# A hybrid decoder step: where the expert router's scores are formed on TensorE and copied on ScalarE

## The reference

```python
q = (xblk @ wq).reshape(PEER_BLOCK, PEER_HEADS, 2, D_HALF)
sc = jnp.einsum('thpc,hpnc->thpn', q, keys)              # scores: 2 x 128 of each token and head
s_top, i_top = lax.top_k(sc, PEER_TOPK)
cand = s_top[..., 0, :, None] + s_top[..., 1, None, :]   # 16 x 16 candidates
best, pos = lax.top_k(cand, PEER_TOPK)                   # the 16 experts
gates = jax.nn.softmax(best, axis=-1)
act = jax.nn.gelu(einsum('thkd,td->thk', u_tab[experts], xblk))
y = einsum('thk,thkd->td', gates * act, v_tab[experts])
```

## Time and profile before

| | us |
|---|---|
| median of 3 runs | 3481.84 |
| lowest to highest | 3478.89 to 3486.58 |
| the profiled execution | 3499.93 |
| its span on the core | 3498.0 |

### The profile page before, as it was taken

How to read it: one execution, slowest core, us unless ns; L and a number is a source line. 1 busy time by engine, 2 the same in 40 slices (tenths; PEclk the granted TensorE clock), 3 DMA queues, 4 the chain that set the end, 5 groups by cost and what they waited for, 6 DMA issues and landing times.

```text
span 3498.0 us, 31532 instructions
## 1 busy us (share of the span) xinstructions
PE 1883.2 (54%) x9976; PEld 885.6 (25%) x9976; DVE 2019.9 (58%) x5131; ACT 705.2 (20%) x1970; POOL 2059.3 (59%) x2211
## 2 busy tenths in 40 slices
PE   6996876766645772644354444444444544444433
PEld 2463543333312220421121111111111211121200
DVE  2337645566677665655655665565566655655563
ACT  2122112221223221112111211121111111111111
POOL 1324546666655555656666666666666666666664
PEclk9998988878766896876676666766666666666666
DMA  9638999999998999989999999999999999999997
GB/s 351 218 111 304 368 331 396 385 391 398 347 376 303 367 369 396 373 331 365 365 359 356 374 365 375 341 372 369 366 361 358 375 362 357 356 369 359 360 363 304
DMA packets 393188, 1228.50 MB, mean 351 GB/s; under 512 B 54563, under 2 KB 104719, under 8 KB 389678
## 3 DMA queue, kind: packets, MB, share of 16 engines
q0 software_dynamic: 305728, 1109.92, 83.6%
q1 hardware_dynamic: 46314, 75.12, 6.1%
q10 hardware_dynamic: 40980, 41.44, 3.6%
HBM read 1211.31 MB, written 16.04 MB: 351 GB/s over the span
## 4 chain that ended last, share of the span: by engine, by line
POOL 33%; issue 20%; another core or an unknown queue 16%; PE 11%; DVE 9%; DMA 7%; ACT 3%; DVEq 2%; ACTq 0%; SPq 0%; POOLq 0%
POOL arena L529 16%; POOL arena L518 16%; DVE arena L1558 5%; DMA arena<-in_peer_v,eid 3%; PE PS L725 3%; DMA arena<-in_peer_u,eid 2%; PE PS L855 2%; PE PS L668 1%; DMA arena<-in_w_ada 1%; PE PS L685 1%; PE PS L825 1%; ACT arena L1171 1%; DMA arena<-in_w_in 1%; PE PS L776 0%
## 5 line engine op out<-in xcount | busy, mean ns | idle before, releaser
L1558 DVE CUSTOM_DVE_ANT_0 arena<-arena,PS 128x1024 f32<-128x1024 f32 x1056 | 1241.9, 1215 | 770.5 <-DMA arena<-in_peer_u,eid 360.6
L855 PE MATMUL PS<-arena 128*32 128x512 f32 x4224 | 853.1, 892 | 1220.0 <-DMA arena<-in_peer_v,eid 754.2
L529 POOL DMA_INDIRECT arena<-in_peer_v,eid x1040 | 982.6, 945 | 840.2 <-remote 366.0
L518 POOL DMA_INDIRECT arena<-in_peer_u,eid x1056 | 998.9, 946 | 408.5 <-issue 313.3
L855 PEld LDWEIGHTS PS<-arena 128*32 128x32 f32 x4224 | 172.3, 141 | 1697.8 <-issue 1549.6
L685 PE MATMUL PS<-arena 128*128 128x256 f32 (+1 forms) x576 | 193.9, 498 | 102.9 <-ACT arena L1047 42.6
L1171 ACT ACTIVATE arena<-sel,wgt 128x32 f32<-128x32 f32 x1056 | 231.0, 310 | 35.5 <-issue 18.9
L1154 ACT ACTIVATE arena<-PS 128x256 f32<-128x256 f32 (+1 forms) x48 | 17.1, 357 | 932.3 <-remote 805.9
L825 PE MATMUL PS<-arena 128*128 128x128 f32 x1280 | 172.5, 293 | 26.2 <-issue 26.2
L825 PEld LDWEIGHTS PS<-arena 128*128 128x128 f32 x1280 | 161.4, 205 | 74.0 <-issue 73.7
L685 PEld LDWEIGHTS PS<-arena 128*128 128x128 f32 x576 | 124.0, 221 | 185.9 <-issue 51.4
(11 more groups left out here) (241 smaller groups left out, 1976.9 us busy)
## 6 DMA issues: line engine op xcount, KB each, us to landing
arena<-in_w_ada SPq DMA_DIRECT2D x24, 1024.0 KB, 11.4
arena<-in_peer_u,eid POOLq DMA_INDIRECT x1056
arena<-in_peer_v,eid POOLq DMA_INDIRECT x1056
arena<-in_peer_wq ACTq DMA_DIRECT2D x10, 1024.0 KB
arena<-in_peer_wq SPq DMA_DIRECT2D x4, 2048.0 KB, 47.7
arena<-in_w_in SPq DMA_DIRECT2D x14, 512.0 KB, 9.8
arena<-in_w_in ACTq DMA_DIRECT2D x14, 512.0 KB
arena<-in_x_prompt ACTq DMA_DIRECT2D x8, 512.0 KB, 5.1
```

The source lines that it names most:

```text
L518: po.indirect_dma_start(out=Ur[:, k % RING, :], out_offset=None, in_=a["peer_u"], in_offset=bass.IndirectOffsetOnAxis(ap=eid[m % 4][:, k:k ...
L529: po.indirect_dma_start(out=Vr[:, k % RING, :], out_offset=None, in_=a["peer_v"], in_offset=bass.IndirectOffsetOnAxis(ap=eid[m % 4][:, k:k ...
L855: last = mm(PS[j * GT:(j + 1) * GT, half, :], dsel[m % 2][:, k, :], rows[:, k % RING, half * 512:(half + 1) * 512], start=m % 2 == 0 and q ...
L1558: last = ve.tensor_tensor_reduce(out=Ur[:, k % RING, :], in0=Ur[:, k % RING, :], in1=hP, scale=1.0, scalar=0.0, op0=ALU.mult, op1=ALU.add, ...
```

## The change

Two lists change, TensorE's and ScalarE's. From unit 24 on TensorE forms the scores of unit n + 2 at the head of its round n, behind the transposes in an even round and ahead of group 0, and no longer between groups 2 and 3. In rounds 22 and 23 they stay where they were. ScalarE copies the scores ahead of the query in every round from 24 on, and no longer behind it; round 23 keeps its order.

```diff
@@ TensorE, round n
                 if n % 2 == 0 and 0 < n < UNITS:
                     replicate(n // 2)
+                if FIRST <= n and n + 2 < UNITS:
+                    scores(n + 2)
                 for q in range(NV):
...
-                    if q == NV - 1 and FIRST <= n + 2 < UNITS:
+                    if q == NV - 1 and n in (FIRST - 2, FIRST - 1):
                         scores(n + 2)
                     if q == NV - 1 and n == FIRST - 1 or q == 1 and n >= FIRST and t < TT:
                         queries(t, h)
@@ ScalarE, round n
-                if n >= FIRST and t < TT:
-                    take_queries(t, h)
                 if FIRST <= n + 2 < UNITS:
                     take_scores(n + 2)
-                if n == FIRST - 1:
+                if n >= FIRST - 1 and t < TT:
                     take_queries(t, h)
                 if n + 1 < UNITS:
                     exps(n + 1)
```

## The result

| | us |
|---|---|
| before, median of 20 runs | 3469.62 (3454.7 to 3486.86) |
| after, median of 20 runs | 3493.04 (3468.13 to 3509.89) |
| ratio, 95% interval | 1.0053 (1.0037 to 1.007) |
| the profiled execution after, its span | 3468.13, 3466.3 |

The change makes the kernel 0.5% slower, some 18 us by the ratio; the two medians lie 23 us apart. The forecast was 3486 with 0.34 on "within 0.2%"; the range of 3430 to 3530 holds the result, and it fell in the case that had 0.37.

The account below looks back on a forecast made before the run. It took a loop of V gather, landing, weighing, late signal and next gather, 92.7 us a pair, as the bound. Terms 0 + 0 + 4 = +4 us on the median 3481.84 gave 3486 us, range 3430 to 3530.

Parts of the forecast that it names:

- the case that had 0.37: Whole kernel: the outcome "slower", beyond the 0.2% counted as the same; its chance was 0.37.
- about 12 us: GpSimd: its waits in each pair of rounds, said to stand ahead of the first of four V gathers.
- ScalarE, 0 us: Scores copy at the head ends the Gelu's 3.5 us lateness, but VectorE still waits for replicated queries: 0 us.
- Rival (c): The Gelu's lateness is on the path, through selectors or U gathers: -40 us, 3442 us, chance 0.16.
- TensorE, where the scores leave, 0 us: Between groups 2 and 3: 1.21 us of scores go, but group 3 waits for its rows anyway: 0 us.
- rival (b): Late signal is held, released by work directly behind group 3: up to 152 us gained, 3330 or 3406 us, chance 0.12.
- TensorE, where they arrive, 0.2 us a pair: Head of the round: gaps hold the scores' 1.21 us; possible signal delay taken as 0.2 us a pair, +4 us.
- 1.6 us a signal: TensorE at the head: upper price of scores behind a group, 13.3 against 11.7 us from start to signal.
- (a): TensorE truly works in the 12 us, so scores delay group 0: +44 us, 3526 us, chance 0.22.
- its two signs: Even rounds: group 0 over 8 us behind the transposes, and waits over 5 us ahead of group 3's V gathers.
- (d): ScalarE's head copy waits for the scores' late signal, but exponentials don't; same result, chance 0.50 together with the forecast.

Follow-up runs that it names:

- e15: Kernel before plus 32 idle matmuls behind each of groups 1, 2 and 3 from round 24 on, on a long-time chip: 3807.47 us, ratio 1.093.
- e3: Changed kernel, but scores at the head in odd rounds only, even rounds as in the kernel before: 3525.57 us, ratio 1.0088 to the kernel before.
- e1: Changed kernel, but in even rounds the scores stand ahead of the transposes: 3529.82 us, ratio 1.0116 to the kernel before.
- e4: Changed kernel, but scores at the head in even rounds only, odd rounds as in the kernel before: 3503.49 us, ratio 1.0039 to the kernel before.
- e5: Kernel before with the scores ahead of group 2 from round 24 on, ScalarE's order unchanged: 3533.19 us, ratio 1.0143.
- e2: Changed kernel with ScalarE's copies in their order of before, on a short-time chip: ratio 1.0001 to the kernel before.
- e9: Changed kernel plus unread matmuls of the scores' size where the scores stood, on a short-time chip: ratio 0.9999 to the kernel before.
- e13: Kernel before with the 16 matmuls of each weighing group run twice from unit 24 on, on a short-time chip: ratio 1.0012.
- e12: Kernel before plus 32 idle matmuls behind each of groups 1, 2 and 3 from round 24 on, on a short-time chip: ratio 1.0001.

## Why the prediction was right or wrong

**What bounds the kernel.** Right in the loop (gather, landing, weighing, late signal, gather) on the chips with long times, open in the cause: "either TensorE still works or its signal is held". Its "about 12 us" of waits sum to 12.9 in its own rows. As far as the rows show, TensorE still works, at a crawl. The kernel after had it in its own rows, the single matmuls at 2786.75 and 2788.85, 2.10 us apart as in e15. Stretches of the kernel after around them:

```profile
2774.00:2782.00 8.00, 4.46 (x40) 1.71 (x32) 0.00 (x0) 0.00 (x0) 6.17 (x7) 0.84 1.02 414
2782.00:2791.00 9.00, 4.71 (x14) 0.87 (x16) 0.01 (x1) 0.00 (x0) 4.11 (x5) 0.77 1.03 411
2791.00:2793.00 2.00, 2.00 (x5) 0.34 (x5) 2.00 (x3) 0.38 (x1) 0.00 (x0) 0.50 0.66 262
2793.00:2795.00 2.00, 2.00 (x10) 2.00 (x11) 1.93 (x9) 0.00 (x0) 1.06 (x2) 0.50 0.00 0
2795.00:2800.00 5.00, 5.00 (x40) 3.92 (x39) 4.85 (x17) 1.25 (x2) 3.20 (x4) 0.79 0.86 261
```

With the DMA share at 1.03 TensorE takes 14 matmuls in 9 us. GpSimd ends its last gather at 2787.47 (2793.64 less the wait of 6.17); 3.5 us later the transposes are out, the DMA engines drain (0.66, then 0.00), and 50 matmuls go in 7 us. In the kernel before GpSimd ends its last gather at 2539.47 - 3.05 = 2536.4, and the transposes are out at 2539.32, 2.9 us later; in e3 it is 3.7 us. So in these three places the signal follows GpSimd's stop by 3 to 4 us, 9.7 or 14.2 us after the group began. This would tell why GpSimd's waits of before are near 3 us each time: a waiting GpSimd feeds the DMA engines nothing, they drain, and TensorE comes free. I read the waits as a price of the signal; they seem to be part of what ends it. This is argued from these rows and from e15.

The prediction cited the Trainium skill, page "Perfetto Trace Analysis", section "Per-instruction lifecycle", for the record's end that is computed. The runs agree: groups with records of 3.6 us are signalled 12 to 13 us after their start. They also show starts that lag inside a group, the one of 2783.50 in the rows above; that this is so because the queue is full is my reading.

**ScalarE, 0 us.** Right, and for the reason given. The Gelu's lateness went, the weights wait 0.27 us, and VectorE stands for the transposes. Rival (c) fell with it. The rule of the Trainium skill, page "TensorE: Matmul & The Clock Gate", section "Architectural detail: the array is 16x 32x32, not 1x 128x128", that ScalarE works strictly in order, agrees with the trace (with the copy ahead, nothing holds the Gelu), and the unblocking was worth nothing.

**TensorE, where the scores leave, 0 us.** This step failed. It priced the gap between groups 2 and 3 by the records (8.66 us idle) and put nothing for group 2's own signal, though rival (b) names it. In even rounds that signal came 3.9 us after the group's start before (mean of 16 readable ones). Now group 2 frees its gather 12.9 us after its start, a wait of 3.3 us above the usual, and 2.0 us on average in the odd rounds of GpSimd. Other groups changed the other way: group 3 of units with an odd number was signalled after 11.0 us and is now after 4.4. So promptness belongs to the place in the rhythm and not to the group. The DMA engines' mean share in the 4 us behind group 2's start went from 0.93 to 1.01, which fits the crawl; no run isolates it.

**TensorE, where they arrive, 0.2 us a pair.** Mis-sized, and for a wrong reason. The transposes come 17.7 us after group 3 instead of 12.6. I had bounded the cost at 1.6 us a signal from one row with the scores behind a group; here it is 5.1 us on one signal. It isn't the scores behind them that do it, since e3 has none there and shows 17.9. What I take for the reason is that GpSimd hardly waits in the even round now (0.44) and goes on issuing until 2787.47, 14.2 us behind the group's start where it was 9.7, so the DMA engines stay full from 2774 to 2791. No run takes that apart.

**Rivals.** (a) was right that TensorE is truly at work, which I argued against with "a weighing of 3.64 us of records can't well be 12 us of work"; its price (44 us) was too high, and of its two signs a wait over 5 us appeared, but ahead of U gathers, while group 0 starts 6.7 us behind the transposes and not over 8. (b) fell: group 3 is sometimes freed sooner (9.5 us in the even round), which is what shrinks the wait to 0.44, and the gain is given back at once at group 2 and the transposes. (d) is what happened on ScalarE: the copy of the scores starts at 2791.15, after 17.37 us of waiting, and the exponentials behind it are in no hurry.

**The sum.** +4 us forecast, some +18 measured. That 3486 lies only 7 us from 3493 is luck: the kernel before came out at 3469.62 and not at 3481.84, 12 us lower, and hid much of the error. Waits of 3 to 6 us a pair went and came and nearly cancel, so the small net is no sign that each step was near zero. What stays open is why the order "between groups 2 and 3" is the best of the six tried (before, after, e1, e3, e4, e5) where TensorE crawls. None of the kernels tried beats the kernel before, and on the chips without the crawl none moves the time by more than 0.12%.

## What to carry to other kernels

Where a signal comes long after the record's end, find out whether the engine is held or works slowly before pricing anything that hangs on it: a filler that keeps it supplied makes the starts of its records tell more. In a loop like this one, in which waits feed back on the DMA traffic, a wait that is removed somewhere fills the DMA engines and comes back elsewhere, so price the loop and not the wait. And run both kernels on more than one chip: here the change costs 0.5 to 0.75% where the kernel before takes some 3480 us, and its two near relatives e2 and e9 cost nothing where it takes 3224. Count the records of a trace too, before a difference between chips is put down to the chip.

## What the runs showed of the hardware

In the experiments the same kernel takes 3485 and 3492 us on two chips and 3222 and 3224 us on two others. The granted clock is not it: 0.67 in the stretch from unit 24 on in the kernel after on a chip with long times, 0.69 in e2 on one with short ones, from these rows:

```profile
1500.00:3000.00 1500.00, 689.18 (x3784) 281.50 (x3788) 889.83 (x2316) 280.83 (x802) 968.15 (x1028) 0.67 0.96 363
```

```profile
1500.00:3000.00 1500.00, 709.72 (x4240) 286.97 (x4232) 992.28 (x2577) 310.49 (x900) 1077.83 (x1146) 0.69 1.02 406
```

VectorE's dots (1216 ns) and the gathers' issue (937 to 945 ns) last the same on both. What differs is how many instructions TensorE takes while the DMA engines are full. Without the crawl the DMA engines are full, 1.02 and 406 GB/s throughout, and GpSimd's issuing alone needs 79.6 of the 83.8 us of a pair; that leaves TensorE room for twice the weighing (1.0012, e13) or 96 more matmuls a round (1.0001, e12) at no cost that matters.
